# The identity products around the second block's delta rule are taken out of TensorE's program

## The reference, cut to what matters

```
for i in range(DEPTH):                       # 2
    hn = rmsnorm(h, ln_mix[i])
    (...) = jnp.split(hn @ w_in[i], SPLIT_POINTS, axis=-1)
    o_gdn = gated_deltanet(...)              # S_t = exp(g_t)(I - beta_t k_t k_t^T) S_{t-1} + beta_t k_t v_t^T
    o_nsa = native_sparse_attention(...)
    o_sb = stick_breaking_attention(...)
    h = h + concat(o_gdn, head_rmsnorm(o_nsa), head_rmsnorm(o_sb)) @ w_out[i]
    h = h + conv_ffn(rmsnorm(h, ln_ffn[i]), w_up[i], ffn_conv[i], w_down[i])
    gate = jax.nn.sigmoid(rmsnorm(h, ln_ple[i]) @ w_ple_gate[i])
    h = h + gate * rmsnorm(p[i] @ w_ple[i], ple_norm[i])
```

## Time and profile before

| what | value |
|---|---|
| time, median of 3 executions | 3974.84 us (3973.45 to 3983.2) |
| the profiled execution's own time | 3975.11 us |
| its span, first to last instruction | 3973.3 us |
| its mean granted TensorE clock | 0.985 of full speed |
| TensorE busy | 3835.5 us, 97% of the span |
| VectorE, ScalarE, GpSimd busy | 59%, 38%, 13% |
| the two mixes lie at | about 2332 to 2548 us and 3281 to 3497 us |

### The profile page before, as it was taken

One profiled execution on the slowest core, in us unless ns is written; L12 is line 12 of the kernel. 1 busy time (PEld: TensorE's weight loads), 2 busy tenths in 40 slices (PEclk: granted clock), 3 DMA queues, 4 the chain that ended last, 5 costly groups with the idle time before them and its releaser, 6 DMA issues. The chain is left out here.

```text
span 3973.3 us, 46667 instructions
## 1 busy us (share of the span) xinstructions
PE 3835.5 (97%) x17822; PEld 3060.2 (77%) x17822; DVE 2334.2 (59%) x3213; ACT 1510.8 (38%) x2185; POOL 509.8 (13%) x366
## 2 busy tenths in 40 slices
PE   8999989999999998999999999999999999999997
PEld 6888658888788875788877677788877767878886
DVE  5445766445544475644467665675567765575656
ACT  3224643223322365422343543343343453343333
POOL 1001721000100055100020012200010002220002
PEclk9999989999999999999999999999999999999999
DMA  4333203333233330333332100122233110022222
GB/s 151 96 97 111 68 16 96 97 100 109 86 96 99 102 96 11 88 96 96 100 108 80 43 22 1 48 96 96 96 108 106 57 39 1 11 80 96 95 96 80
DMA packets 87019, 315.01 MB, mean 79 GB/s; under 512 B 10016, under 2 KB 10400, under 8 KB 86176
## 3 DMA queue, kind: packets, MB, share of 16 engines
q1 hardware_dynamic: 83664, 302.43, 24.3%
q10 hardware_dynamic: 3152, 9.74, 0.8%
HBM read 307.94 MB, written 2.10 MB: 78 GB/s over the span
## 5 line engine op out<-in xcount | busy, mean ns | idle before, releaser
L383 ACT ACTIVATE wh<-raw 128x1024 fp32r<-128x1024 f32 x564 | 597.5, 1059 | 1630.8 <-PE ps L403 1317.1
L401 PE MATMUL ps<-xh,wh 128*128 128x512 f32 x2336 | 917.9, 393 | 15.9 <-DVE xl L466 9.2
L402 PE MATMUL ps<-xl,wh 128*128 128x512 f32 x2336 | 910.9, 390 | 0.0
L403 PE MATMUL ps<-xh,wl 128*128 128x512 f32 x2336 | 910.7, 390 | 0.0
L387 DVE TENSOR_TENSOR wl<-raw,wh 128x1024 fp32r<-128x1024 f32 x564 | 696.2, 1234 | 182.0 <-ACT wh L383 181.1
L401 PEld LDWEIGHTS ps<-xh,wh 128*128 128x128 f32 x2336 | 439.8, 188 | 112.3 <-issue 19.8
L402 PEld LDWEIGHTS ps<-xl,wh 128*128 128x128 f32 x2336 | 439.9, 188 | 94.1 <-issue 3.6
L403 PEld LDWEIGHTS ps<-xh,wl 128*128 128x128 f32 x2336 | 439.8, 188 | 91.9
L401 PE MATMUL ps<-fh,wh 128*128 128x512 f32 x1016 | 397.1, 391 | 4.0 <-DVE wl L387 4.0
L402 PE MATMUL ps<-fl,wh 128*128 128x512 f32 x1016 | 395.4, 389 | 0.0
L403 PE MATMUL ps<-fh,wl 128*128 128x512 f32 x1016 | 395.4, 389 | 0.0
(11 more groups left out here) (465 smaller groups left out, 5568.5 us busy)
## 6 DMA issues: line engine op xcount, KB each, us to landing
raw<-in_w SPq DMA_DIRECT2D x564, 512.0 KB, 3.5
con<-in_consts SPq DMA_DIRECT2D x1, 2053.5 KB, 14.0
h<-in_x SPq DMA_DIRECT2D x4, 512.0 KB, 7.0
p_t<-in_p ACTq DMA_DIRECT2D x4, 512.0 KB, 4.3
w1k<-in_w1c ACTq DMA_DIRECT2D x2, 1024.0 KB, 4.8
w1v<-in_w1c ACTq DMA_DIRECT2D x2, 1024.0 KB, 6.9
out<-h SPq DMA_DIRECT2D x8, 256.0 KB, 2.1
dup_k<-roped ACTq DMA_DIRECT2D x8, 128.0 KB, 3.4
```

The lines of the kernel that those rows point to most:

```text
L383: nc.scalar.activation(wh[k % 2][:, :], raw[k % 4][:, :], ACT.Copy).then_inc(s["w_hi"], 1)
L401: nc.tensor.matmul(DB[k % 2][:, :], a, hi(q), start=(q == order[0]), stop=False)
L402: nc.tensor.matmul(DB[k % 2][:, :], a, lo(q), start=False, stop=False)
L403: last = nc.tensor.matmul(DB[k % 2][:, :], b, hi(q), start=False, stop=(q == order[-1]))
```

## The change

The function `pe_idle` and its seven calls are removed. The semaphore waits that stood ahead of two of the calls stay where they were, ahead of `pe_uw`. Nothing is added or moved, and no other engine's program differs.

```
-        def pe_idle(bank, at_, count):
-            for _ in range(count):
-                nc.tensor.matmul(bank[:, at_:at_ + P], c("ident"), c("ident"), start=True, stop=True)
...
                     for i in range(3, PIECES):
                         pe_pre(pe, s, 0, i)
-                    pe_idle(DB[0], 0, 14)
                     pe_sb(pe, s, 1)
...
                                     pe.wait_ge(s["s_state"], 6 * t)
                                 else:
                                     pe.wait_ge(s["eg_ready"], 1)
-                                pe_idle(BK[2], 0, 8)
-                        if not more:
-                            pe_idle(BK[0], 0, 4)
                         pe_uw(pe, s, t)
-                    pe_idle(BK[0], 0, 8)
                     pe_out(pe, s, 2, 0)
...
                             pe_values(pe, s, ITEMS - 1)
-                            pe_idle(T_BANK, 0, 6)
                             post(len(posted) - 1)
-                            pe_idle(T_BANK, 0, 7)
                             pe.wait_ge(s["post_done"], len(posted))
```

## The result

The kernel without the identity products took 3992.1 us (median of 4 executions, 3989.0 to 4000.2); the kernel before took 3974.1 us on the same chip. The ratio is 1.0048, 95% interval 1.0036 to 1.0060: slower by more than 0.3%. The forecast was 3983.0 us, and no change as the likeliest outcome; the time lies just inside the stated range, which ended at 3993. The profiled execution took 3989.3 us, its span is 3987.5 us and its mean clock 0.978.

A forecast was written before the change was run, and what follows sets the result against it. TensorE, busy 97% of the span, was taken as the bound. Per layer -1.5 (overruns) + 2.3 + 2.3 (clock falls) + 1.0 (tail) = +4.1, both layers +8.2 us: 3983.0 us, range 3975.0 to 3993.

The forecast's parts named there:

- A: 6 filler products before the projections' last transposes: gain 0.03 us; with B even odds of a clock fall, 0 or 2.3 us.
- B: 7 filler products before the mix: gain 0.03 us; with A even odds of a clock fall, 0 or 2.3 us.
- C: 14 filler products before level 1: gain 0; the wait grows to 5.45 us and the clock falls, costing 2.3 us per layer.
- D: 8 filler products before the u/w products of t = 0: overrun, gain 0.75 us; clock fall three times in ten.
- E: 8 filler products before the u/w products of t = 1: overrun, gain 0.75 us; clock fall three times in ten.
- F: 4 filler products before the u/w products of t = 2: no gain, possibly a loss of 0.1 us.
- G: 8 filler products before the last `pe_out`: gain 0 us, at most 0.36, because VectorE is the bound there.
- the tail: From the last u/w products to the output projection: clock falls some 10 us earlier, costing 1.0 us per layer (0 to 2).
- Rival 3: Delta rule's narrow products don't bring the clock back: long half clock, +10.8 us per layer, 3996.7 us; chance 0.20.
- Rival 5: Fall at A and B certain, as transposes between them keep the clock no more than a wait: 3985.3 us; chance 0.10.
- Rivals 1, 2 and 4: Only C falls, 3976.7 us (0.14); clock holds everywhere, 3972.1 (0.05); D's and E's gain doesn't arrive, 3986.0 (0.05).

The follow-up runs named there:

- C alone: Only the 14 filler products at C removed from the kernel before, all other places kept: 3982.4 us, ratio 1.0017.
- D and E at 3: The kernel before with the filler at D and E cut from 8 to 3 products each: 3976.9 us, ratio 1.0002.
- the early filler: The kernel before with A and B removed and 14 more 128-row products early in the preparation, C kept: 3990.9 us, ratio 1.0035.

## Why the prediction was wrong

The prediction was right in that the clock, and not the instructions, decides, and in the direction of every term. One term, the price of a fall at A and B, was three times too small, and that carried the time past 0.3%. The stretch up to the last u/w products was forecast about 3 us longer per layer, and was 8.0 and 6.4 us longer. Step by step:

- *The instructions themselves.* Forecast: A, B and C free, D and E 0.75 us each, F +0.1. With D to G removed and the clock up, the levels (which end at D's place) took 51.82 us, 0.80 less; the next stretch, which ends at E's place, 62.54, 0.72 less; in the changed kernel too it is 62.55, and F's stretch 43.45, +0.07. Right.
- *The price of half clock.* 0.47 us for each microsecond at half clock: the preparation went from 9.95 to 18.15 us, 8.20 / 18.15 = 0.45. Right for work without a gap. The Trainium skill's gaps (TensorE: Matmul & The Clock Gate, "Back-to-back issue gap") gave 0.49; for this mixed work the trace gives less.
- *C.* Forecast: a fall in its wait and 2.3 us. C alone gave +2.5 and +2.7 in the levels. Right for C by itself. In the changed kernel it is not a fall of its own: the clock was already down, and the levels lost 1.48 + 0.75 = 2.2 and 1.5 us to the same stretch at half clock.
- *A and B: the step that failed.* "Even odds of a fall, at 0 or 2.3 us." The clock fell in both layers, and the stretch from the preparation to level 1 grew by 7.1 and 6.3 us. The 2.3 was 5 us at half clock, taken from the durations behind ten long waits; 27 and 24 us were measured, 4.4 of them in C's wait. What follows here is a preparation made largely of 64-row products, and those don't raise the clock (30.11 us at 0.50). The text looked at what stood behind C's wait and at the narrowness of the levels, and not at what stands behind A and B. The better row was in it: 11.57 us at half clock from 505.20, on narrow attention products.
- *D and E.* A fall three times in ten each: none in the changed kernel. That odds were due is shown by the kernel with only A and B, whose clock fell behind D's place in both layers (67.04 us where 62.54 stand without a fall, +4.5).
- *F, G and the tail.* Forecast +1.0 (0 to 2), measured +1.9 and +0.9. That it came so near is in part luck: the price was put at 0.11 us for each of 10 us more at half clock; it was 7 and 3 us more, at about 0.27 us each. The tail with D and E at 3 shows that this price depends on where the half clock lies.

Set right, the layer is -1.5 + 0.1 + 6.7 + 1.9 + 1.4 = +8.6 (means of the two layers), 17.1 for both; the medians differ by 18.0.

*The rivals.* Rival 3 had the mechanism, narrow products that don't bring the clock back, but put it into the levels; it lies ahead of them, and level 1, with products of 128 rows, had it back after 3 to 5 us. Its 3996.7 us is 4.6 us off, the forecast 9.1 (the 1.5 us in the rival's sum has no working, and neither has the +19 us of the range); the rival's reading of the earlier trace rows was the better one, though its place was wrong. Rival 5 had the event, a fall at A and B in both layers, for a wrong reason: transposes do keep the clock up. That the Trainium skill's rule (same page, "Part 4: PE-mode transpose") does not hold for these transposes is shown twice, as filler at A and B (15.48 us) and at C (52.62 us, where 64-row products gave 54.45). Rivals 1, 2 and 4 fell: the short waits at A and B did not leave the clock up, and D's and E's gain arrived.

*What stays open.* Why a wait is followed by a fall in one kernel and not in another. The wait of 2.13 us before level 1 is harmless before and was not with the early filler; the 2.4 us one of the PLE products was followed by a fall once D and E were shorter; the 0.83 us one before the u/w products was followed by one with only A and B kept, and not in the changed kernel nor with A, B and C kept. A chance of a fall is what such a row gives, and which of these it will be was not found.

Nor was it tried how much 128-row work among other work is enough to raise the clock, or whether tiles of 64 columns count as 64 rows do. The filler shows only what pure 64-row and pure 128-row products do. Two rows say that more than the rows matters. With only A and B kept, the u/w products (all 128 rows, but tiles of 64 in another direction) ran at half clock from 2406.05 to 2412.25, and the clock came back about 4 us into the full tiles of level 1 behind them. And of the ten falls that the prediction read, one of the three long ones, from 545.65, came before products 512 wide and not before attention. With C removed that stretch lasted until 563.46. TensorE was busy for 18.63 of its 20.48 us, and only 4 of them were products of 64 rows (the groups of 547.66 and 554.97). Two runs of 2.8 us each of products of 128 rows and 512 columns lie in it, each with attention behind it; the clock came back in the third run, 4.0 us after its start:

```profile
544.83 0.76 PE L807 MATMUL ps<-p_hi,wh 128*128 128x512 f32 x1 [4.62 <-DVE e_t L1178]
...
547.66 2.07 PE L821 MATMUL ps<-k_t,q_t 64*128 64x256 f32 x4
...
559.45 0.77 PE L807 MATMUL ps<-p_hi,wh 128*128 128x512 f32 x1
```

## What to carry to other kernels

Filler in a wait is worth what the clock costs behind that wait, so look first at what follows it. Here the full tiles of the levels lost 2 to 3 us, the u/w products with tiles of 64 columns 4.5, and a run mostly of 64-row products kept losing until full-row work came, 7 us. Two short waits with little work between them (0.66 us) brought a fall that neither brought alone; filling either was enough. Make filler of full rows, and no longer than its wait: D and E overran theirs by 0.75 us each, while the unfilled waits of the first block were worth 9 us. And look at both ends of an edit: what it gives in one stretch can go into the clock of the next.

## What the runs showed of the hardware that was not expected

- A stretch of 30.11 us in which TensorE was busy without a gap, mostly with products of 64 rows, was at 1.2 GHz (0.50); 14 products or 14 transposes of 128 rows brought it back within the filler.
- The same 64-row products kept a full clock up (13 of them at A and B, 15.83 us of preparation). To hold the clock and to raise it are different things.
- Identical code has different stretches at half clock from one execution to the next. Behind the first block's wait of 4.62 us for the copy of a PLE product it was 10.24 us in the profiled execution before and 20.48 us in the one with C removed, although the two programs are the same up to there. Single executions of the kernel before lie up to 13 us apart (3971.9 to 3985.0 in 16), and their mean clocks go with it (0.986 to 0.982). So the half clock of one profile outside the place of the change says nothing about the change.

Before, and with C removed:

```profile
544.08:554.32 10.24, 8.67 (x25) 0.50 0.20 54
```

```profile
542.98:563.46 20.48, 18.63 (x52) 0.50 0.07 27
```
